# Second layer's expert-norm shift and scale computed behind the first layer's overflow, its gate behind the latent products

## The reference

```
mod = silu(cond) @ w_mod[l] + b_mod[l]            # w_mod[l] is 1024 x 6144
sh1, sc1, g1, sh2, sc2, g2 = split(mod, 6)
x = x + g1 * mixer(rmsnorm(x, norm_mix[l]) * (1 + sc1) + sh1)
h = rmsnorm(x, norm_ffn[l]) * (1 + sc2) + sh2     # "expert norm"
x = x + g2 * moe(h)                               # 16 experts, two per token
```

## Time and profile before

| what | us |
|---|---|
| median of 3 runs | 959.93 |
| lowest and highest | 952.76, 964.01 |
| the profiled execution | 958.43 |
| its span | 956.6 |
| busy in the span: PE, DVE, ACT, POOL | 798.8, 378.3, 271.0, 95.1 |
| mean granted TensorE clock | 0.914 |

### The profile page before, as it was taken

How to read it: one execution, slowest core, us unless ns; L and a number is a source line. 1 busy time by engine, 2 the same in 40 slices (tenths; PEclk the granted TensorE clock), 3 DMA queues, 4 the chain that set the end, 5 groups by cost and what they waited for, 6 DMA issues and landing times.

```text
span 956.6 us, 11465 instructions
## 1 busy us (share of the span) xinstructions
PE 798.8 (84%) x4035; PEld 440.2 (46%) x4035; DVE 378.3 (40%) x844; ACT 271.0 (28%) x631; POOL 95.1 (10%) x146
## 2 busy tenths in 40 slices
PE   4879999999879987999771779878899989998750
PEld 0237665635434555555330445545554565554320
DVE  3376673354253341421113434664643334221114
ACT  1242112210541231222112325555532322221111
POOL 3200000001000013000004002211200030000002
PEclk8589999999989996999995779999999969999995
DMA  9991174369960287999997936202115589999965
GB/s 287 368 330 46 44 175 140 119 232 322 310 247 0 69 315 247 401 411 411 411 374 244 375 100 256 90 1 90 46 46 219 196 321 399 413 410 412 389 246 197
DMA packets 85055, 232.21 MB, mean 243 GB/s; under 512 B 7188, under 2 KB 17101, under 8 KB 84681
## 3 DMA queue, kind: packets, MB, share of 16 engines
q1 hardware_dynamic: 72706, 193.89, 55.6%
q0 software_dynamic: 8576, 27.38, 8.6%
q10 hardware_dynamic: 3720, 10.25, 2.9%
HBM read 216.60 MB, written 17.78 MB: 245 GB/s over the span
## 4 chain that ended last, share of the span: by engine, by line
PE 58%; DMA 17%; DVE 8%; issue 7%; SPq 4%; ACT 3%; DVEq 2%; POOLq 1%; POOL 0%; ACTq 0%
PE ps L868 52%; DMA ring<-in_moe_w_up_dram 7%; PE ps L875 4%; DMA arena<-in_moe_w_up_dram 3%; SPq L654 2%; DMA ring<-in_w_mod_dram 2%; PE ps L1095 2%; DVEq L1842 1%; SPq L637 1%; DVE negmax L1895 1%; DMA h_rows<-xn 1%; DMA arena<-y_rows,rows_out 1%; DMA hT<-h_rows,rows_in 1%; DVE xn L2286 1%; ACT hT L1557 1%
## 5 line engine op out<-in xcount | busy, mean ns | idle before, releaser
L868 PE MATMUL ps<-arena 128*64 128x256 f32 (+13 forms) x1084 | 229.4, 453 | 30.1 <-DMA arena<-in_moe_w_down_dram 7.5
L868 PEld LDWEIGHTS ps<-arena 128*64 128x64 f32 (+4 forms) x1084 | 123.5, 171 | 119.6 <-issue 67.0
L868 PE MATMUL ps<-ring,hT 128*128 128x512 f32 (+2 forms) x384 | 134.5, 509 | 6.5 <-issue 5.9
L868 PE MATMUL ps<-ring,arena 128*64 128x256 f32 (+1 forms) x864 | 126.1, 435 | 15.0 <-DMA ring<-in_moe_w_up_dram 7.3
L868 PEld LDWEIGHTS ps<-ring,hT 128*128 128x128 f32 x384 | 73.2, 193 | 64.2 <-issue 59.8
L868 PEld LDWEIGHTS ps<-ring,arena 128*64 128x64 f32 x864 | 60.9, 137 | 65.0 <-issue 39.3
L875 PE MATMUL ps<-ident,arena 128*128 128x128 f32 (+2 forms) x332 | 50.6, 292 | 21.1 <-DVE hT L1901 5.6
L1514 ACT ACTIVATE arena<-ps 128x256 f32<-128x256 f32 (+5 forms) x88 | 38.7, 454 | 94.1 <-PE ps L868 87.5
L2226 DVE TENSOR_TENSOR arena<-arena,ps 128x128 f32<-128x128 f32 x37 | 10.7, 288 | 133.3 <-ACT arena L1619 133.3
L868 PE MATMUL ps<-hT,ring 128*128 128x384 f32 x192 | 62.1, 486 | 0.0
L868 PE MATMUL ps<-ring,condT 128*32 128x512 f32 x384 | 53.1, 682 | 7.6 <-DMA ring<-in_w_mod_dram 6.9
(11 more groups left out here) (295 smaller groups left out, 833.6 us busy)
## 6 DMA issues: line engine op xcount, KB each, us to landing
ring<-in_w_mod_dram SPq DMA_DIRECT2D x48, 1024.0 KB, 8.8
ring<-in_moe_w_down_dram SPq DMA_DIRECT2D x24, 1024.0 KB, 17.8
ring<-in_moe_w_gate_dram SPq DMA_DIRECT2D x42, 512.0 KB, 14.0
ring<-in_moe_w_up_dram SPq DMA_DIRECT2D x42, 512.0 KB, 16.3
arena<-in_moe_w_gate_dram SPq DMA_DIRECT2D x32, 512.0 KB, 8.5
arena<-in_moe_w_up_dram SPq DMA_DIRECT2D x32, 512.0 KB, 10.2
arena<-in_moe_w_down_dram SPq DMA_DIRECT2D x13, 1024.0 KB, 13.3
ring<-in_ev_w_in_dram SPq DMA_DIRECT2D x9, 1024.0 KB, 13.1
```

The costliest lines, as they stand in the source:

```text
L868: mm = pe.matmul(out, lhsT, rhs, **kw)
```

## The change

The "mla" chunks are ordered `sh2`, `sc2`, `g1`. The four chunks of `sh2` and `sc2` (`MOD_AHEAD = 4`) are multiplied on TensorE right after the overflow loop, before the first turn of the second layer, into banks 3, 5, 7 and 3. Their eight pieces are sent ahead of the two pieces of `od_w_in`. ScalarE copies and stores the first row between its scaling of tile 0 and tile 1, and the other three after the modulation of tile 2, before its first copy of a latent product. GpSimd moves the four rows before it stores the latent state. VectorE sums all four at the end of head group 0. The first chunk of `g1` is multiplied right behind the latent products, and ScalarE copies it before the square root of the latent norm. The second chunk with the first's selection comes at the end of group 1, the second's selection at the end of group 2. Nothing is left behind the first projections or at the end of group 0. What is computed is the same.

```diff
--- before.py
+++ after.py
@@ -75,14 +75,15 @@
     "start": halves((0, SH1), (0, SC1)),
     "gqa": halves((0, SH2), (0, SC2), (1, SH1), (1, SC1), (0, G1)),
     "ffn0": halves((0, G2)),
-    "mla": halves((1, G1), (1, SH2), (1, SC2)),
+    "mla": halves((1, SH2), (1, SC2), (1, G1)),
     "ffn1": halves((1, G2)),
 }
 MOVED = [chunk for where in CHUNKS for chunk in CHUNKS[where] if chunk[1] not in (G1, G2)]
 MODA_ORDER = [(0, 0), (0, 1), (1, 0), (1, 1)]
 MLA_NORM_STEPS = 7
 MLA_NORM_AT = {0: 0, 1: 1, 2: 2, 3: 3, 5: 4, 6: 5, 7: 6}
-MLA_AHEAD = 3
+MOD_AHEAD = 4
+MOD_BANKS = (3, 5, 7, 3)
 MLA_PAIRS = [(0, 0), (0, 1), (1, 0), (2, 0), (1, 1), (2, 1)]
 MLA_KEYS = (3, 1, 2)
 NPAIRS = NT * QH // 2
@@ -257,13 +258,14 @@
     B.stage("gL", 2 * NT, (7,))
     B.stage("gO", NT, (6,))
     moe_stage(0)
+    for i in range(MOD_AHEAD):
+        mod_stage("mla", i, [MOD_BANKS[i]] * 2)
     B.stage("hT1.0", 2 * NT, (0, 1, 2, 4, 0, 1))
     B.stage("um", NT, (6, 7))
+    mod_stage("mla", MOD_AHEAD, [5, 5])
     B.stage("cT", NT + 1)
     B.stage("mq0", NT)
     B.stage("mk0", NT + 1)
-    for i in range(MLA_AHEAD):
-        mod_stage("mla", i, BANK_M)
     for g in range(NHG):
         B.stage(f"mv{g}", NT + 1, (2, 3, 4, 5))
         B.stage(f"mqT{g}", NT, (0, 1, 2))
@@ -275,7 +277,8 @@
         B.stage(f"mPT{g}", 2 * len(MLA_PAIRS), (4, 5))
         B.stage(f"mO{g}", 2, (6,))
         B.stage(f"mL{g}", 4, (7,))
-        mod_stage("mla", MLA_AHEAD + g, (0, 1))
+        if g:
+            mod_stage("mla", MOD_AHEAD + g, (0, 1))
     moe_stage(1)
 
 
@@ -286,8 +289,8 @@
         at[name] = len(pieces)
         pieces.append([(src, 0, shape, slice(0, P))])
 
-    def mod_pieces(where):
-        for l, v, half in CHUNKS[where]:
+    def mod_pieces(where, chunks=slice(None)):
+        for l, v, half in CHUNKS[where][chunks]:
             c0 = v * D + half * 512
             for kh in range(2):
                 w = d["w_mod"][l].rearrange("(p j) n -> p j n", j=KT)
@@ -340,10 +343,11 @@
     mod_pieces("gqa")
     out_pieces(0, d["ev_w_out"][0])
     moe_pieces(0)
+    mod_pieces("mla", slice(0, MOD_AHEAD))
     od_in = d["od_w_in"][0].rearrange("(p j) n -> p j n", j=KT)
     for kh in range(2):
         piece(f"in1.{kh}", od_in[:, 4 * kh:4 * kh + 4, :], 4, ODD_IN)
-    mod_pieces("mla")
+    mod_pieces("mla", slice(MOD_AHEAD, None))
     out_pieces(1, d["od_w_out"][0])
     moe_pieces(1)
 
@@ -825,6 +829,8 @@
                 load(pool, in_mla, head_gain[:, 0:1], d["od_q_norm"].rearrange("a n -> n a"))
                 load(pool, in_mla, head_gain[0:NOPE, 2:3], d["od_k_norm"][:, 0:NOPE].rearrange("a n -> n a"))
                 load(pool, in_mla, ropem, d["rope_m"].rearrange("p (a b c) -> p a b c", b=2, c=ROPE))
+                for i in range(MOD_AHEAD):
+                    move_row("mla", i)
                 pool.wait_ge(lora_ready, 1)
                 pool.dma_start(st_ckv[0, 0], um[:, 0, QR:QR + KVR]).then_inc(stored, 16)
                 pool.dma_start(st_kr[0, 0], um[:, 0, QR + KVR:]).then_inc(stored, 16)
@@ -836,7 +842,6 @@
                         pool.drain()
                         rope(pool, q4[:, t, :, NOPE:QK], qtab[:, t - 1, :, :], mrb[:, 0, :, :], mrb[:, 1, :, :], HG, ROPE)
                     pool.drain().then_inc(qk_turned, 1)
-                    move_row("mla", MLA_AHEAD - 1 + g)
             pool.wait_ge(stored, 16 * 4)
 
 
@@ -1040,7 +1045,8 @@
                     if i == 6:
                         mla_values(g, 0)
                 mla_sums_turn(g, 1)
-                mod_step("mla", MLA_AHEAD + g)
+                if g:
+                    mod_step("mla", MOD_AHEAD + g)
                 mla_values(g, 1)
                 mla_sums_spread(g, 1)
 
@@ -1428,12 +1434,17 @@
             moe(0)
 
 
+            for half in range(2):
+                pe.wait_ge(y_read[half][0], NE)
+            for i in range(MOD_AHEAD):
+                mod_step("mla", i)
             mixer_turn(1, 0)
             latent_in(0)
             mixer_turn(1, 1)
             mixer_turn(1, 2)
             latent_in(1)
             latent_in(2)
+            mod_step("mla", MOD_AHEAD)
             pe.wait_ge(lora_ready, NT)
             loaded(pe, in_mla)
             for t in range(NT + 1):
@@ -1465,8 +1476,6 @@
                     fill_inc(mm, f"{stage}{g}", t)
 
             project(0)
-            for i in range(MLA_AHEAD):
-                mod_step("mla", i)
             for g in range(NHG):
                 project_kv(g, "mv", NOPE)
                 pe.wait_ge(qk_ready, NT + 1 + g)
@@ -1786,6 +1796,7 @@
 
             act.activation(statA[:, 1, 0:1], statA[:, 0, 0:1], ACT.Sqrt)
             scale_first(0, 0)
+            mod_step("mla", 0)
             scale_first(0, 1)
             next_norm(0)
             scale_first(0, 2)
@@ -1795,12 +1806,15 @@
             next_norm(2)
             for t in range(1, NT):
                 modulate_tile(1, 0, t, "hT1.0", 2 * t)
+            for i in range(1, MOD_AHEAD):
+                mod_step("mla", i)
             for t in range(NT):
                 copy_out("um", t, um[:, t, :], bank_of("um", t)[:, 0:ODD_IN])
                 act.drain()
                 act.activation(junk[:, t, 0:QR], um[:, t, 0:QR], ACT.Square, accum_out=statA[:, 0, t:t + 1])
                 ins = act.activation(junk[:, t, QR:QR + KVR], um[:, t, QR:QR + KVR], ACT.Square, accum_out=statA[:, 0, NT + t:NT + t + 1])
             ins.then_inc(lora_sq, 1)
+            mod_step("mla", MOD_AHEAD)
             act.wait_ge(lora_var, 1)
             act.activation(statA[:, 1, 0:2 * NT], statA[:, 0, 0:2 * NT], ACT.Sqrt).then_inc(lora_root, 1)
             for t in range(NT + 1):
@@ -1816,10 +1830,7 @@
                              bank_of(f"mk{g}", t)[:, 0:HG * NOPE].rearrange("p (h e) -> p h e", h=HG))
 
             queries_keys(0)
-            mod_step("mla", 0)
             mla_root(0)
-            for i in range(1, MLA_AHEAD):
-                mod_step("mla", i)
             for g in range(NHG):
                 for t in range(NT + 1):
                     copy_out(f"mv{g}", t, v4[:, t, :, :], bank_of(f"mv{g}", t)[:, 0:HG * VD].rearrange("p (h e) -> p h e", h=HG))
@@ -1940,7 +1951,9 @@
                     if g + 1 < NHG and i in MLA_NORM_AT:
                         mla_norm(g + 1, MLA_NORM_AT[i])
                 mla_mask(g, 1)
-                mod_step("mla", MLA_AHEAD + g)
+                if g == 0:
+                    for i in range(1, MOD_AHEAD + 1):
+                        mod_step("mla", i)
                 mla_join(g, 1)
 
             def pair_max(i):
```

## The result

| | before | after |
|---|---|---|
| median of 4 runs, us | 960.61 | 973.74 |
| lowest, highest | 952.76, 964.01 | 969.43, 975.18 |
| profiled execution | 958.43 | 969.43 |
| its span | 956.6 | 967.6 |
| PE busy | 798.8 | 805.6 |

The ratio is 1.0129 (95%: 1.009 to 1.0168): 1.3% slower, clear of the noise. (The quotient of the two medians is 1.0137.) The profiled execution after is the fastest of its four. The two profiled ones lie 11.0 us apart, the medians 13.1. The four executions after have spans of 967.6, 970.8, 973.0 and 973.3 us at mean clocks of 0.923, 0.915, 0.911 and 0.907: most of their scatter goes with the clock.

The account below looks back on a forecast made before the run. It took the bound as the chain of waits from first-layer experts to second-layer attention, its long pieces TensorE's, with the gathers critical in the filled hole. Eight terms summed to +10.9 us: 958.43 to 969.3, range 959 to 977.

Parts of the forecast that it names:

- 1 first latent product: Tile 0's latent product starts late, as weight pieces share the queues with the store and gathers: +5.0 us, ends +3, +7.
- 2 its clock: Tile 0's latent product keeps most of its cold start: -0.5 us, ends -2.1 and 0.
- 3 bank 7: Tile 1's latent product waits until ACT has copied the third modulation product from bank 7: +2.9 us, up to +3.5.
- 4 behind bank 7: Tiles 1 and 2: cold clock after TensorE's empty 3.4 us, overlapping ACT's late copies: +1.5 us, ends 0 and +3.1.
- 5 gate before the root: Behind the latent products, ACT's gate copy precedes the square root the latent norm awaits: +1.9 us.
- 6 clock of turns, projections: Behind the latent products, a shorter hole may keep the clock up for turns and projections: -1.0 us, ends -3.9, 0.
- 7 three products gone: Behind the first projections, removing 11.8 us of TensorE work wins little: 0, ends -2.0 and +1.5 us.
- 8 group ends: Products and selections rearranged at the ends of the head groups: -1.9, +3.0 and +0.1, given as +1.1 us.
- A: Rival: clock holds through the gaps of 3.4 and 3.5 us and comes up early in tile 0: 964.0, chance 0.15.
- B: Rival: all late ends, with half-rate gathers, slow store and cold clock after every gap: 976.5, chance 0.17.
- C: Rival: faster, the first latent product not late, eighth piece by 527, last gather by 522: 957.0, chance 0.13.
- the prediction's signs: Trace signs, among them four products of 16 matmuls on TensorE between 504 and 534, at clock 0.50.

Follow-up runs that it names:

- the stream alone: Kernel before, with seven modulation weight pieces sent ahead of SyncE's wait for the gathers and no product moved: ratio 1.0047.
- three other profiles of the same order: Changed kernel with ScalarE's copies of rows 2 to 4 before modulating tiles 1 and 2, its gate copy behind the square root, or both: 1.0047, 1.0092, 1.0044.
- the gate's mend alone: Changed kernel, with ScalarE's copy of the gate's first row moved behind the square root of the latent norm: ratio 1.0092.
- the gate product alone: Kernel before, with only the gate's first product moved into the hole behind the latent products, its copy behind the root: ratio 0.9956.
- the two together: Kernel before, with the gate's first product behind the latent products and three group-end products inside attention: 951.63 us against 961.06, ratio 0.9913.
- both mends: Changed kernel, with rows 2 to 4 copied ahead of modulating tiles 1 and 2 and the gate's row behind the root: ratio 1.0044.
- the rows early: Changed kernel, with ScalarE's copies and stores of rows 2 to 4 ahead of its modulation of tiles 1 and 2: ratio 1.0047.

## Why the prediction was right

The time came out 4.4 us above the forecast of 969.3, inside the range of 959 to 977. Half of the 4.4 is the base: the forecast counted from the profiled execution, 2.2 us under the median of 960.61. The mechanisms were right: late gathers, the bank, the cold clock behind it, the root, and next to nothing for the work taken off TensorE. That +10.9 was forecast and that the profiled executions lie 11.0 apart is in part luck, as the terms show, each from the same two profiles:

| step | predicted | measured | from |
|---|---|---|---|
| ahead of the change | 0 | +0.5 | down product ends 505.05, was 504.51 |
| 1 first latent product | +5.0 | +5.6 | 538.92, was 532.83, less the 0.5 |
| 2 its clock | -0.5 | -0.3 | 7.52, was 7.79 |
| 3 bank 7 | +2.9 | +3.4 | tile 1 starts 5.8 after tile 0's end, was 2.4 |
| 4 behind bank 7 | +1.5 | +1.7 | 13.11, was 11.41 |
| 5 gate before the root | +1.9 | +1.6 | root 3.4 after the products, was 1.8 |
| 6 clock of turns, projections | -1.0 | +0.2 | turns to norm 10.90, was 10.68 |
| 7 three products gone | 0 | -1.2 | norm to projections 16.05, was 17.21 |
| 8 group ends | +1.1 | +1.0 | to output projection 124.7, was 123.7 |
| behind | 0 | -1.5 | output projection to the end |

To the output projection this is +12.5 against the +10.9 of the sum. The last line is in no part of the change. The stretch behind the start of the output projection took 244.6 us here and 245.2 to 250.9 in the nine other profiles that run it unchanged (246.1 in the one of before), so the -1.5 that brings the 12.5 near the forecast is the scatter of one execution.

*Step 1* was right in kind, and the experiments carry it: the stream alone gives the same 33.9 us. Its size was right in this one profile. The three other profiles of the same order have 7.1, 7.5 and 9.4 us over the kernel before at this point, past the upper end of +7, and by the path of the eighth piece, which the prediction had only 3.1 late. Two of them then ran the latent product at full clock (5.8 us), so that at its end they are 5.5 and 7.5 us later than the kernel before, the third 6.9, and the changed kernel's own profile 5.3 (each counted from the end of the down product). The two paths that I set side by side, by bytes and by gathers, ended within 1.3 us of each other: ScalarE's part of tile 0, on the path of the eighth piece, at 537.55, VectorE's part, on the path of the third join, at 538.8. The eighth piece came at 532.9, not 530.3: from 500 to 533 the mean rate was 395 GB/s, not 412, and small loads of GpSimd's moved beside it. The gathers' path came as worked out: with the 0.5 of the start taken off, the third join began at 531.9. The rule of the Trainium skill in "DMA: Bandwidth & Descriptors", "Queues, rings and completion order" gave 5.5 for this term. The trace agrees for the path of the gathers: 5.6, the six gathers stretched from 12.3 to 17.4 us, and to 17.2 to 17.4 in the four other profiles with the whole stream beside them.

*Step 2.* Nearly right in number, for another reason than given: the product didn't start cold. The clock was up at 536 and fell at about 539.5, inside the product, as it fell inside those of tiles 1 and 2, 0.9 us after they began. In two of the three other profiles of this order it didn't fall in the product at all, which is the term's other end (-2.1).

*Steps 3 and 4* were named with their mechanism (ScalarE's order), and undoing it brought back 2.4 and 11.41 us. With the order left as it was, the gate's mend alone showed the wait of 4.0 us and the 13.11 again. In step 4 the part that counted was the clock alone: the store of the second row had landed by 555.29 after ScalarE had waited 3.33 us for it, the latent copy of tile 0 was done at 557.04, and the 32 matmuls of tiles 1 and 2 are one unbroken run.

*Step 5* came to 1.6, and moving the copy behind the root takes the 1.6 away each time. *Step 6* gave the warm clock a quarter of its 3.9 us. Here it gave nothing: the clock fell again while TensorE stood empty for 3.21 us. With a wait of 1.64 us instead, it held up to the norm in one profile of four (7.1 us from the turns to the norm), and fell inside the turns or the projections in the other three (8.8 in the gate product alone and in the two together, 9.8 in both mends). With the longer wait and the rows early it was 9.8 too. So the shorter wait gave back the warm turns (ten in 1.31 us three times and in 1.64 once, for 2.35 to 2.40); that it keeps the clock up isn't shown, nor is what the place of the gate is worth in the whole.

*Step 7.* The stage won 1.2 us, inside its ends of -2.0 and +1.5, and in the way the prediction had it: the turns began 10.8 us after the norm instead of 14.1 (3.3 won), but at low clock, 5.42 us instead of 3.24 (2.2 back). GpSimd's rotation, for which the prediction had TensorE wait a second time, held nothing up: the 28 turns are one unbroken run behind VectorE's norm. The core of the forecast came true all the same: to take 11.8 us of work off TensorE, the change paid some 12 us in steps 1 to 6 and got 1 back.

*Step 8* came out as worked out, but for a slip of a tenth: -1.9, +3.0 and +0.1 are +1.2, not +1.1. In the three other profiles of this order the groups took 124.4 to 127.6 us, so the +1.0 is one reading.

*Rivals.* A (clock holds, 964.0) failed at both gaps. B (all late, 976.5) is as near to the median of 973.74 as my sum is, but not by its terms: the bank's wait was near its end (3.4 of 3.5), the first product (5.6 of 7), the cold clock (1.7 of 3.1) and the turns (-1.2 of +1.5) were not, in the profiled execution. In the three other profiles of this order the first product was all late. C (faster, 957.0) asked for the eighth piece by 527 and the last gather by 522; they came at 532.9 and 530.5. Of the prediction's signs, one failed: the clock wasn't 0.50 all through the four products, whose first three halves took 1.06 to 1.21 us, at full clock.

Open: what makes the 2.1 us between the medians' distance (13.1) and that of the profiled executions (11.0). Two things point the same way: the profiled one has the shortest rest behind the output projection of all, and the earliest first latent product of its order. No run parts them.

## What to carry to other kernels

A hole on TensorE isn't free when transfers are what it waits for: filling it with work that brings 8.4 MB of weights delays the very gathers that end the hole. Here they started 2.9 us later and took 5.1 us longer, and in three profiles of four the last piece of those weights came later still. Before moving work into a hole, ask what fills the queues during it, and where in another engine's order the results will be copied out; here the wrong places of four small copies on ScalarE cost more (0.85 points of the ratio) than the transfers (0.47). Work that needs no new transfer and is copied behind what is awaited (the gate's product in the later hole, the group-end products inside attention) did pay: 0.9% together.

## What the runs showed of the hardware

The granted clock fell within attention in some stretches and not in others. In the profile of the kernel with the gate product alone, the same four score matmuls took:

```profile
593.24 2.36 PE L869 MATMUL ps<-arena 96*128 96x384 f32 x4
...
627.99 1.46 PE L869 MATMUL ps<-arena 96*128 96x384 f32 x4
```

2.36 us in one group, where the clock fell (0.82 in the slice from 593, then 0.50), and 1.46 at full clock in another. Its groups took 126.7 us where the kernel before took 123.7, though nothing in them was changed, and that execution took 964.11 us, 6 above the median of its runs. A single profile of this kernel can be off by more than the effects studied here. Nor does a short wait make the clock safe: behind one of 1.64 us it held up to VectorE's norm in one profile (28 projections in 7.56 us) and fell in three, in both mends with 10.12 us for the same 28.

A store of 256 KB, 2.9 us on an empty queue, took 5.9 beside the weight stream (506.1 to 512.0), and one row of 16 KB 4.9 (550.34 to 555.29). A sixteenth of the bytes took nearly the same time: beside the stream it wasn't the transfer's own bytes that set it in these two.
